# Sparse attention: the compressed scores move from one batch to the score groups of heads 0 to 7, and all weight transposes use the transpose operation

## The reference, cut to what matters

```
s_c = einsum('bghqd,bgcd->bghqc', qb, k_cmp) + dense_bias(d_c)      # 15 compressed keys
p_c = masked_softmax(s_c, d_c >= 0)
o_c = einsum('bghqc,bgcd->bghqd', p_c, v_cmp)
...
s_s = einsum('bghqd,bgqnld->bghqnl', qb, k_sel) + bias_s            # selected blocks
p_s = masked_softmax(s_s, d_s >= 0);  o_s = p_s @ v_sel
s_w = einsum('bghqd,bgkd->bghqk', qb, k_w) + dense_bias(d_w)        # window
p_w = masked_softmax(s_w, mask_w);    o_w = p_w @ v_w
y = sum(gates * [o_c, o_s, o_w] * silu(z))
out = y @ out_w
```

## Time and profile before

| what | us |
|---|---|
| median of 3 runs | 1188.27 |
| lowest and highest of them | 1181.31, 1189.44 |
| the profiled execution, its own time | 1185.39 |
| its span in the trace | 1183.6 |

### The profile page before, as it was taken

How to read it: one execution, slowest core, us unless ns; L and a number is a source line. 1 busy time by engine, 2 the same in 40 slices (tenths; PEclk the granted TensorE clock), 3 DMA queues, 4 the chain that set the end, 5 groups by cost and what they waited for, 6 DMA issues and landing times. The chain is left out here.

```text
span 1183.6 us, 17327 instructions
## 1 busy us (share of the span) xinstructions
PE 1087.5 (92%) x7300; PEld 973.0 (82%) x7300; DVE 700.4 (59%) x1009; ACT 572.9 (48%) x846; POOL 102.3 (9%) x94
## 2 busy tenths in 40 slices
PE   2699998899978999998998999999998969999997
PEld 2599897798867877887996789899887968998996
DVE  5678774775465665476543445545555885555544
ACT  3355546633554455345335645334435675444344
POOL 0100028260000001122000001000000200000000
PEclk9999999999989999799898999999999989999999
DMA  9766335442336852203454025555553525555551
GB/s 327 227 186 178 107 107 179 142 143 83 107 107 216 286 173 72 72 1 107 143 178 142 1 89 190 184 180 182 192 193 114 172 78 171 182 183 195 188 178 71
DMA packets 118349, 178.43 MB, mean 151 GB/s; under 512 B 5156, under 2 KB 78018, under 8 KB 118272
## 3 DMA queue, kind: packets, MB, share of 16 engines
q1 hardware_dynamic: 116736, 172.40, 45.2%
q0 software_dynamic: 1120, 2.97, 0.8%
q10 hardware_dynamic: 416, 1.97, 0.4%
HBM read 176.27 MB, written 1.05 MB: 150 GB/s over the span
## 5 line engine op out<-in xcount | busy, mean ns | idle before, releaser
L1191 DVE TENSOR_TENSOR sb_w_lo<-sb_raw,sb_w_hi 128x2048 fp32r<-128x2048 f32 (+2 forms) x141 | 320.3, 2272 | 275.9 <-ACT sb_w_hi L605 275.7
L605 ACT ACTIVATE sb_w_hi<-sb_raw 128x2048 fp32r<-128x2048 f32 (+2 forms) x141 | 266.2, 1889 | 200.0 <-PE G L1954 145.0
L1952 PE MATMUL X<-sb_hT_hi,sb_w_hi 128*128 128x256 f32 x1056 | 303.4, 287 | 13.5 <-DVE sb_hT_lo L1516 9.1
L1954 PE MATMUL X<-sb_hT_hi,sb_w_lo 128*128 128x256 f32 x1056 | 300.8, 285 | 0.0
L1953 PE MATMUL X<-sb_hT_lo,sb_w_hi 128*128 128x256 f32 x1056 | 300.7, 285 | 0.0
L1952 PEld LDWEIGHTS X<-sb_hT_hi,sb_w_hi 128*128 128x128 f32 x1056 | 204.5, 194 | 16.7 <-DVE sb_hT_lo L1516 9.8
L1953 PEld LDWEIGHTS X<-sb_hT_lo,sb_w_hi 128*128 128x128 f32 x1056 | 204.6, 194 | 0.8
L1954 PEld LDWEIGHTS X<-sb_hT_hi,sb_w_lo 128*128 128x128 f32 x1056 | 204.5, 194 | 0.0
L1952 PE MATMUL G<-sb_w_hi,sb_hT_hi 128*128 128x512 f32 x256 | 104.5, 408 | 11.7 <-DVE sb_hT_lo L1906 9.5
L1952 PE MATMUL G<-sb_w_hi,sb_uT_hi 128*128 128x512 f32 x256 | 101.4, 396 | 0.0
L1953 PE MATMUL G<-sb_w_lo,sb_uT_hi 128*128 128x512 f32 x256 | 101.2, 395 | 0.0
(11 more groups left out here) (404 smaller groups left out, 1625.8 us busy)
## 6 DMA issues: line engine op xcount, KB each, us to landing
sb_raw<-in_mlp_w SPq DMA_DIRECT2D x64, 1024.0 KB, 5.4
sb_raw<-in_ada_w SPq DMA_DIRECT2D x24, 1024.0 KB, 5.3
sb_raw<-in_a_in_w SPq DMA_DIRECT2D x16, 1024.0 KB, 5.9
sb_raw<-in_b_in_w SPq DMA_DIRECT2D x16, 1024.0 KB, 5.9
sb_raw<-in_sb_w_qkv SPq DMA_DIRECT2D x12, 1024.0 KB, 5.2
sb_raw<-in_rg_w_in SPq DMA_DIRECT2D x8, 1024.0 KB, 5.8
sb_raw<-in_a_out_w SPq DMA_DIRECT2D x4, 1024.0 KB, 5.0
sb_raw<-in_b_out_w SPq DMA_DIRECT2D x4, 1024.0 KB, 5.1
```

Source lines behind the costliest of these rows:

```text
L605: nc.scalar.activation(w_hi[s][:, 0:nk * w], raw[b % RAW_SLOTS][:, 0:nk * w], ACT.Copy).then_inc(S["w_hi"], 1)
L1191: nc.vector.tensor_tensor(w_lo[s][:, 0:nk * w], raw[b % RAW_SLOTS][:, 0:nk * w], w_hi[s][:, 0:nk * w].bitcast(F32), ALU.subtract).then_inc ...
L1952: dt32(out, lh, rh, start=first, stop=False, skip_group_check=shared)
L1954: return dt32(out, ll, rh, start=False, stop=last, skip_group_check=shared)
```

## The change

TensorE's `scores(h)` for h < 8 gets four products of 15 columns more: the compressed scores of heads h and h+8 for both halves of the tokens, into columns 384 to 413 of bank G0 (head h) or G1 (head h+8). The batch after head 8 is gone. VectorE adds their bias in two instructions of 30 columns behind the `nmx` of each of the heads 0 to 7, and `scores(h)` waits for it as well. The shift, the exponentials, the scale, the turning and the products of the compressed branch come one head earlier each. `weights_T` uses the transpose operation for all 16 heads. The wait for the compressed keys moves ahead of `scores(0)`, and the wait for the last z tiles into `c_weights_T`.

```diff
--- before.py
+++ after.py
@@ -998,10 +998,10 @@
                     split_for(first_mm["b_z"] + 8 + Z_SPLITS.index(h))
                 if h + 2 < BH:
                     head_exp(h + 2)
-                if h == 10:
+                if h == 9:
                     act.wait_ge(S["c_arg"], 1)
                     nc.scalar.activation(pc[:, :, :, :], pc[:, :, :, :], ACT.Exp).then_inc(S["c_exp"], 1)
-                if h == 12:
+                if h == 11:
                     act.wait_ge(S["c_tr"], 1)
                     nc.scalar.activation(pcT, G[2][0:8 * NCMP, :], ACT.Copy).then_inc(S["c_trs"], 1)
             y1_hi(0)
@@ -1618,6 +1618,17 @@
                                                                ALU.add, ALU.max, mx[:, h % 2, i:i + 1]))
                 ch.settle()
                 nc.vector.tensor_scalar(nmx[:, h % 2, :], mx[:, h % 2, :], -1.0, None, ALU.mult).then_inc(S["nmx"], 1)
+                if h < 8:
+                    c_scores(h)
+
+            def c_scores(first):
+
+                for h in (first, first + 8):
+                    ins = nc.vector.tensor_tensor(pc[:, :, h, :], G[h // 8][:, 3 * P:3 * P + MT * NCMP]
+                                                  .rearrange("p (q n) -> p q n", q=MT), bias_cmp[:, :, h, :], ALU.add)
+                    if h < 8:
+                        ch.mark(ins)
+                ins.then_inc(S["c_bias"], 1)
 
             def gated_heads(h2):
 
@@ -1649,23 +1660,12 @@
                 nc.vector.scalar_tensor_tensor(sz_of(j, t), sz_of(j, t), 1.0, G[2 + t][:, :], ALU.add, ALU.mult)\
                     .then_inc(S["z_out"], 1)
 
-            def c_scores():
-
-                dve.wait_ge(S["c_score"], 2)
-                for q in range(MT):
-                    for odd in range(2):
-                        src = G[2 + odd][:, q * 8 * NCMP:(q + 1) * 8 * NCMP].rearrange("p (h n) -> p h n", h=8)
-                        ins = nc.vector.tensor_tensor(pc[:, q, odd:BH:2, :], src, bias_cmp[:, q, odd:BH:2, :], ALU.add)
-                        if (q, odd) != (1, 1):
-                            ch.mark(ins)
-                ins.then_inc(S["c_bias"], 1)
-
             flat = pc[:, :, :, :].rearrange("p q h n -> p (q h) n")
             cfac = cmx[:, :, :].rearrange("p q h -> p (q h)")
 
             def c_shift():
 
-                dve.wait_ge(S["c_bias"], 1)
+                dve.wait_ge(S["c_bias"], 8)
                 ch.settle()
                 ch.link(nc.vector.tensor_reduce(cmx[:, :, :], pc[:, :, :, :], AX, ALU.max))
 
@@ -1728,16 +1728,14 @@
                     if h % 4 == 0:
                         factors(h // 4 - 1)
                 if h == 9:
-                    c_scores()
+                    c_shift()
                 if h == 10:
-                    c_shift()
-                if h == 11:
                     c_scale()
-                if h == 13:
+                if h == 12:
                     dve.wait_ge(S["tm_out"], 5)
                     dve.wait_ge(S["z_out"], 2)
                     c_gated(0)
-                if h == 14:
+                if h == 13:
                     c_gated(1)
             y1_lo(0)
             gated_heads(BH // 2 - 1)
@@ -2415,17 +2413,30 @@
             def scores(h):
                 if h >= 1:
                     pe.wait_ge(S["nmx"], h)
+                    pe.wait_ge(S["c_bias"], min(h, 8))
                 r, g = half_rows(h), h // 8
                 for br in range(2):
                     bank = G[br]
                     dt32(bank[:, 0:P], qB[r, h // 2, 0:P], kdup[br][r, g, 0:P], start=True, stop=True)
                     ins = dt32(bank[:, P:3 * P], qB[r, h // 2, P:T], kdup[br][r, g, :], start=True, stop=True)
+                if h < 8:
+                    ins = c_scores(h)
                 ins.then_inc(S["s_head"], 1)
+
+            def c_scores(first):
+
+                for h in (first, first + 8):
+                    for q in range(MT):
+                        o = 3 * P + q * NCMP
+                        ins = dt32(G[h // 8][:, o:o + NCMP], qB[half_rows(h), h // 2, q * P:(q + 1) * P],
+                                   kc_T[half_rows(h), h // 8, :], start=True, stop=True)
+                return ins
 
             def first_scores():
 
                 pe.wait_ge(S["fm_out"], 19)
                 pe.wait_ge(S["tm_out"], 2 + 3)
+                pe.wait_ge(S["cmp_k"], 2)
                 scores(0)
 
             for b in range(4):
@@ -2461,7 +2472,6 @@
                     ins.then_inc(S["cmp_rep"], 1)
             scores(1)
             gate_rows(24)
-            pe.wait_ge(S["cmp_k"], 2)
             pe.wait_ge(S["vbd"], 2)
 
             def z_piece(p):
@@ -2482,20 +2492,10 @@
 
             z_split = []
 
-            def c_scores():
-
+            def c_weights_T():
+
+                pe.wait_ge(S["c_arg"], 2)
                 pe.wait_ge(S["z_out"], 6)
-                for q in range(MT):
-                    for h in range(BH):
-                        o = (q * 8 + h // 2) * NCMP
-                        ins = dt32(G[2 + h % 2][:, o:o + NCMP], qB[half_rows(h), h // 2, q * P:(q + 1) * P],
-                                   kc_T[half_rows(h), h // 8, :], start=True, stop=True)
-                        if q == 1 and h >= BH - 2:
-                            ins.then_inc(S["c_score"], 1)
-
-            def c_weights_T():
-
-                pe.wait_ge(S["c_arg"], 2)
                 for q in range(MT):
                     for g in range(BG):
                         ins = transpose(G[2][0:8 * NCMP, (2 * q + g) * P:(2 * q + g + 1) * P],
@@ -2521,7 +2521,7 @@
                 for br in range(2):
                     for i in range(3):
                         piece = TB[br][:, i * P:(i + 1) * P], pr[h % 2][:, br, i * P:(i + 1) * P], ident
-                        ins = transpose(*piece) if h < 8 else dt32(*piece, start=True, stop=True)
+                        ins = transpose(*piece)
                 ins.then_inc(S["p_tr"], 1)
 
             def head_out(h):
@@ -2564,16 +2564,14 @@
                     scores(h + 2)
                 if h < 8:
                     z_piece(2 * h + 1)
-                if h == 12:
+                if h == 11:
                     c_weights_T()
-                if h in (13, 14):
-                    c_out(h - 13)
+                if h in (12, 13):
+                    c_out(h - 12)
                 if h == BH - 1:
                     pe.wait_ge(S["nmx"], BH)
                     y1_transposes(0)
                 head_out(h)
-                if h == 8:
-                    c_scores()
 
             def y1_second():
```

More of the change, by code:

```diff
@@ L2483, in _ @@
             z_split = []
-            def c_scores():
-                pe.wait_ge(S["z_out"], 6)
-                for q in range(MT):
-                    for h in range(BH):
-                        o = (q * 8 + h // 2) * NCMP
-                        ins = dt32(G[2 + h % 2][:, o:o + NCMP], qB[half_rows(h), h // 2, q * P:(q + 1) * P],
-                                   kc_T[half_rows(h), h // 8, :], start=True, stop=True)
-                        if q == 1 and h >= BH - 2:
-                            ins.then_inc(S["c_score"], 1)
             def c_weights_T():
                 pe.wait_ge(S["c_arg"], 2)
+                pe.wait_ge(S["z_out"], 6)
                 for q in range(MT):
```

## The result

The changed kernel takes 1198.98 us in the median of 4 runs (1198.02 to 1202.59). The kernel before, on the same chip, took 1187.7 (4 runs, 1181.31 to 1189.44). The ratio is 1.0125, with a 95% interval of 1.0084 to 1.0165: 1.25% slower. The forecast was 1178, the range 1170 to 1192; both are missed.

A forecast was written before the change was run, and what follows sets the result against it. The prediction took the head loop as bound by TensorE, with a chain through VectorE and ScalarE close behind. Its terms, -5.9 - 5.7 - 5.6 + 7.2 + 1.4, made -8.6 us, hence 1178 us, range 1170 to 1192.

The forecast's parts named there:

- The low clock goes with the batch: Head loop behind the removed batch: 12.4 us at the low clock return to the high one, -5.7 us.
- If TensorE finds its next work ready: Condition on the -5.6 us from transposes in heads 8 to 15: TensorE must not wait for other engines.
- 5.9 us of cost: Batch of compressed scores after head 8: removing it was booked as -5.9 us.
- the clock falls anyway: Rival, heads 8 on: transposes leave too little arithmetic, clock low; 1191 until head 12 (chance 0.12), 1206 whole loop (0.06).
- Eight more records a head: Heads 0 to 7: eight 15-column records on one partition half add 0.9 us a head, +7.2 us, bounds 3.5 and 7.4.
- the small products are cheap: Rival, heads 0 to 7: 15-column records cost 0.055 us each even on one half, -3.6, 1174 us; chance 0.12.
- Transposes of heads 8 to 15: Turning weights by six transposes instead of twelve identity records saves 0.7 us a head, -5.6 us.
- Waits at heads 10, 11 and 14: TensorE waits from moving the compressed branch one head earlier: 0.7, 0.1 and 0.7 us, net +1.4 us.
- The small adds: VectorE's two 30-column adds in heads 0 to 7: 0.35 us for both, covered by TensorE's other work, cost nothing.
- rivals of the chain: Rival, heads 8 to 15: longer handovers keep the period near 4.5 us, transposes bring nothing, +5.6, 1184 us; chance 0.14.
- exposed adds: Rival, heads 0 to 7: TensorE's wait for the small adds is exposed, +2.8, 1181 us; chance 0.04.
- two anchors: Starting points for the forecast: profiled execution's 1185.39 gives 1176.8, the runs' median 2.9 higher gives 1179.7; 1178 lies between.

The follow-up runs named there:

- experiment 3: The changed kernel with the last z-weight split moved from head 8 to head 11: 1179.24 us, ratio 0.9953; run again on another chip, 1178.07, ratio 0.9943.
- experiment 2: The kernel before, batch included, with transposes for the weights of all 16 heads and nothing else changed: 1193.21 us, ratio 1.0075.
- experiment 5: The changed kernel with the last split at head 11, plus a useless 2.3 us VectorE subtraction at head 8: 1192.58 us, ratio 1.0068.
- experiment 6: The changed kernel with 16 useless fp32r products of 256 columns on TensorE ahead of `head_out` of head 9: 1186.41 us, ratio 1.0005.
- experiment 7: The changed kernel with VectorE's `factors(1)` (0.9 us) at head 9 in place of head 8: 1187.01 us, ratio 1.0022.
- experiment 10: The changed kernel with identity products for the weights of heads 10 and 11 alone, transposes everywhere else: 1183.97 us, ratio 0.9981.
- experiment 1: The changed kernel with the weights of heads 8 to 15 turned by identity products again, 12 records a head: 1184.7 us, ratio 0.9992.
- experiment 4: The changed kernel with both the last split at head 11 and identity products in heads 8 to 15: 1183.25 us, ratio 0.9961.
- experiment 9: The changed kernel with the split at head 11 and ScalarE's compressed exponentials behind its copy of head 10, not head 9's: 1177.67 us, ratio 0.9951.

## Why the prediction was wrong, and where it was right

**The low clock goes with the batch (-5.7): the step that failed.** It said "This holds if the fall was the batch's doing and nothing in the new order brings one", and something did. The low stretch grew from 17.07 to 47.79 us. Of the 21.6 us by which the loop missed its 32.9, the clock made 20.4 (experiment 3 against the changed kernel).

**"If TensorE finds its next work ready": the step under it.** I went through the duties of the compressed branch that move and found waits at heads 10, 11 and 14. I left out what lies in head 8 already and does not move: split, `gated_heads` and `factors`, 3.7 us in a row on VectorE. The batch was named as 5.9 us of cost, and it was also 5.9 us of cover. I asked what each moved piece would wait for, and not what the removed work had covered. The wait was 2.05 us by itself. With what it set off it costs 1198.98 - 1179.24, 20 us (18 if each median is first taken against the kernel before beside it: 11.3 above and 7.2 below).

**The rival "the clock falls anyway"** was right in its kind: 1206 with the whole remaining loop at 0.50, against 1199. It priced 28 us where the clock took 20.4, since the loop's first 9.6 us (488.12 to 497.73) were still at 1.00. Its factor for a head at the low clock holds: heads 10 and 11 of experiment 2 take 6.9 us each (497.62 to 504.50 to 511.39), 1.89 times the 3.64, where it had 1.86. What was wrong was the cause given: "the new work would hardly raise it sooner" is shown (3.41 us of low clock with identity products, 47.79 without), but transposes alone don't bring it down (experiment 3, 1.00 throughout). The row that I held against the rival, 16 transposes in 1.80 us that left the clock at 1.00, stands, but it could not answer the question: it shows that transposes leave a high clock high, not that they bring a low one back. The two are different, and I took one for the other. The rival should have had two conditions, a fall and no return, with the batch's fall as proof that this loop falls easily. (The Trainium skill, page "TensorE: Matmul & The Clock Gate", section "Part 4: PE-mode transpose", says that transposes don't count as activity for the full clock. For the return of the clock the traces agree, with 40.96 us against 17.07 in experiment 2. By the same rule the loop of experiment 3 might be expected to fall, and it doesn't.)

**Eight more records a head (+0.9 each, +7.2).** Nearly right. The eight records take 0.89 us from start to start, and a head grew by 0.81 (7.24 - 6.43). From the first scores to head 8, with all eight groups in between, it is 68.38 - 62.04 = 6.3 us; the other 0.5 of the 6.9 by which head 8 starts later lies ahead of the first small product. The step that small products on one half of the partitions cost as much as `head_out`'s records holds: 0.11 each. The rival "the small products are cheap" is out. That alternating halves would halve this was not tried; in the batch, neighbours lay in different banks as well as on different halves, and no run separates the two.

**Transposes of heads 8 to 15 (-5.6).** Right in TensorE's busy time (36.76 to 31.16). In the loop's length 4.6 are left, since waits grow by 1.0, which the prediction had as +1.4 in a term of its own.

**Waits at heads 10, 11 and 14 (0.7, 0.1, 0.7).** 0.60, none and 0.97 in experiment 3. The small adds cost no wait in heads 0 to 7: TensorE is busy for all 68.38 us there. The rivals of the chain and of the exposed adds are out as well: head 8 took 3.64 us, not 4.5, and heads 8 and 9 of experiment 3, whose starts are at 491.26, 494.90 and 498.74, took 3.64 and 3.84. The two small adds take 0.28 us together, where I had 0.35.

**The sum.** Head 8's start 6.9 later and a loop of 32.87 in place of 48.67 make -8.9, where the prediction had -8.6. So the arithmetic is that of a kernel with the last split three heads later, which differs from the kernel as it was changed by a single wait that was not on the list. That its medians, 1179.24 and 1178.07, come out so near the 1178 is in part luck: against the kernel before beside them they are 7.2 and 6.8 us lower, not 8.6, and the 1178 was a middle between two anchors.

**What stays open.** Why the clock comes back under the first `c_out` in some executions (the traces of experiments 5 to 7) and under neither of the two in others (the changed kernel) isn't settled: the same four records of 512 columns were there each time, 3.4 to 3.8 us long. The kernel before has such a spread too, 1178 to 1194 us in 31 runs, and one of its executions has a trace. Not all of the spread comes from the loop: the two traced executions of the kernel of experiment 3 have the same loop of 32.87 us, but head 8 starts at 491.26 in one and at 487.75 in the other, with a granted clock of 0.91 and 0.95 between 300 and 400 us. Nor is it settled from what length on a wait brings the fall: a fall followed those of 0.89, 1.32, 1.76, 1.96 and 2.05 us; none followed those of 0.60 and 0.97 in experiment 3 (two `c_out` lie shortly before the second), that of 1.26 in experiment 7 by itself, or that of 2.05 in experiment 10. What the traces of the new order do show together: with a wait of 0.89 us or more at head 9 or 10, five of six executions had a fall there (the changed kernel and experiments 1, 5, 6 and 7, but not 10); with at most 0.60 us there, none of four had one (experiments 3, twice, 4 and 9).

## What to carry to other kernels

Work that is taken off the bounding engine was also cover. Before you book it as a gain, write down what every other engine does underneath it, with its special duties of that very step (here a split, gates and factors in a row in head 8, which cost nothing in head 4, where z pieces lie over them), and see which of them is late when it is gone. In a stretch of small float32 records, a wait of two microseconds cost about twenty here, because it may take the clock down and what follows may not bring it back. Work that looks wasteful, such as turning by a product with the identity, can be what brings it back (3.41 us of low clock with it in experiment 1, 47.79 without); ask of each clock fall separately what starts it and what ends it. Of the versions here the change with the last split at head 11 is the best, 0.5 to 0.6% below the kernel before (1179.24 and 1178.07), and experiment 9's variant of it can't be told apart from it. Its cure was to spread out the duties of one head.

## What was unexpected of the hardware

- TensorE stayed at 1.2 GHz for 47.79 us while it was busy for 47.09 of them, in a row of float32 transposes, scores and products of 64 columns, and with two `c_out` of four records of 512 columns in it, 3.78 us each:

```profile
516.09 3.78 PE L2511 MATMUL G<-sb_vbd,sb_tpair 120*128 120x512 f32 x4
...
526.39 3.78 PE L2511 MATMUL G<-sb_vbd,sb_tpair 120*128 120x512 f32 x4
...
542.59 0.77 PE L1950 MATMUL G<-sb_w_hi,sb_hT_hi 128*128 128x512 f32 x1
```

  It came back only 2.93 us into the output projection, which begins at 542.59.
- Falling and returning are not the same. With the same TensorE instructions the clock stayed at 1.00 through the whole loop (experiment 3), and, once it had fallen in head 10's transposes, at 0.50 to the loop's end (the changed kernel). In experiments 5 to 7 it came back in the first `c_out`.
- A fall followed a wait of only 0.89 us in such a stretch (experiment 6), and under the 64 products of 15 columns it came with no wait at all (experiment 2). A wait of 2.05 us was once followed by none (experiment 10).
- A record of 15 columns on half of the partitions takes 0.11 us, the step of the records of 64 columns in `head_out`, where its neighbours are on the same half and mostly in the same bank. In the batch, with neighbours on the other half and in the other bank, it was 0.055.
